# The expert loop's phase: the way down first, and the last block's hidden rows turned inside the way down before it

## The reference, cut to what matters

```python
x = x + concat(pool_mix(z), conv_mix(z)) @ w_out + b_out
h = rms_norm(x)
# the best of 4 expert groups, then the best 2 of its 8 experts; rows sorted into blocks of 128 per expert
yb = (silu(xblk @ w_eg[e]) * (xblk @ w_eu[e])) @ w_ed[e]      # per block: 128x1024 -> 512 -> 1024
y.at[buf_tok].add(yb * gate)
out = rms_norm(x + y)
```

## Time and profile before

| what | us |
|---|---|
| median of 3 runs | 1068.87 (1068.7 to 1072.86) |
| the profiled execution, its own time | 1070.19 |
| its span in the trace | 1068.4 |
| PE busy | 945.7 (89%) |
| DVE busy | 865.0 (81%) |
| ACT busy | 635.7 (59%) |
| POOL busy | 293.1 (27%) |

### The profile page before, as it was taken

How to read it: one execution, slowest core, us unless ns; L and a number is a source line. 1 busy time by engine, 2 the same in 40 slices (tenths; PEclk the granted TensorE clock), 3 DMA queues, 4 the chain that set the end, 5 groups by cost and what they waited for, 6 DMA issues and landing times.

```text
span 1068.4 us, 13431 instructions
## 1 busy us (share of the span) xinstructions
PE 945.7 (89%) x4446; PEld 774.7 (73%) x4446; DVE 865.0 (81%) x967; ACT 635.7 (59%) x623; POOL 293.1 (27%) x324
## 2 busy tenths in 40 slices
PE   4999999896898783969999999999999999999920
PEld 3888888574687563758888888888888888888720
DVE  6289998969756646889889898989898989898658
ACT  7244453563531103648787878787878787878515
POOL 2178688375153101002121212121212121212010
PEclk8999999897998875879999999999999999999965
DMA  8221111121351142579999999999999999999877
GB/s 265 82 61 40 40 40 45 37 104 45 133 217 60 69 153 90 214 262 368 379 377 390 389 391 383 402 384 384 384 392 372 384 384 374 380 385 384 296 248 273
DMA packets 67531, 268.63 MB, mean 251 GB/s; under 512 B 15359, under 2 KB 28159, under 8 KB 42921
## 3 DMA queue, kind: packets, MB, share of 16 engines
q1 hardware_dynamic: 57993, 250.36, 63.0%
q0 software_dynamic: 9504, 17.85, 4.4%
HBM read 254.09 MB, written 30.86 MB: 267 GB/s over the span
## 4 chain that ended last, share of the span: by engine, by line
PE 84%; DVE 6%; ACT 3%; DMA 3%; issue 3%; POOL 1%; SPq 0%; DVEq 0%; POOLq 0%; ACTq 0%
PE ps L1076 11%; PE ps L1074 11%; PE ps L1075 11%; PE ps L925 8%; PE ps L1088 6%; PE ps L1090 6%; PE ps L1089 6%; PE ps L801 5%; PE ps L802 5%; PE ps L803 5%; PE ps L1063 3%; PE ps L980 2%; PE ps L1095 1%; PE ps L839 1%; DMA arena<-hm_scratch,g_idx 1%
## 5 line engine op out<-in xcount | busy, mean ns | idle before, releaser
L726 ACT ACTIVATE big<-arena 128x2048 fp32r<-128x2048 f32 x192 | 362.5, 1913 | 70.4 <-PE ps L1090 38.6
L1525 DVE TENSOR_TENSOR low<-arena,big 128x2048 fp32r<-128x2048 f32 x126 | 285.2, 2285 | 39.8 <-ACT big L726 39.8
L1074 PE MATMUL ps<-big,ring 128*128 128x512 f32 x512 | 204.4, 399 | 2.4 <-DVE ring L1530 2.4
L1076 PE MATMUL ps<-big,ring 128*128 128x512 f32 x512 | 202.4, 395 | 0.0
L1525 DVE TENSOR_TENSOR big<-arena,big 128x2048 fp32r<-128x2048 f32 x66 | 151.0, 2289 | 16.5 <-ACT big L726 16.2
L1208 DVE SCALAR_TENSOR_TENSOR ps<-arena,cols,ps 128x512 f32<-128x512 f32 (+1 forms) x174 | 137.2, 788 | 6.0
L925 PE MATMUL ps<-big,ring 128*128 128x512 f32 (+1 forms) x432 | 113.4, 423 | 14.0 <-DVE ring L1274 7.1
L1074 PEld LDWEIGHTS ps<-big,ring 128*128 128x128 f32 x512 | 96.9, 189 | 22.1 <-DVE ring L1530 2.8
L925 PEld LDWEIGHTS ps<-big,ring 128*128 128x128 f32 (+1 forms) x432 | 84.6, 199 | 38.6 <-DVE ring L1274 7.5
L1076 PEld LDWEIGHTS ps<-big,ring 128*128 128x128 f32 x512 | 96.9, 189 | 21.2
L1088 PE MATMUL ps<-big,hT 128*128 128x512 f32 x256 | 103.0, 402 | 10.1 <-DVE hT L1540 10.1
(11 more groups left out here) (240 smaller groups left out, 1394.7 us busy)
## 6 DMA issues: line engine op xcount, KB each, us to landing
arena<-in_w_eg SPq DMA_DIRECT2D x64, 1024.0 KB, 7.5
arena<-in_w_eu SPq DMA_DIRECT2D x64, 1024.0 KB, 7.2
arena<-in_w_ed SPq DMA_DIRECT2D x64, 1024.0 KB, 7.6
arena<-in_x_prompt SPq DMA_DIRECT2D x16, 512.0 KB, 4.5
y_in<-y_scratch SPq DMA_DIRECT2D x16, 512.0 KB, 7.8
arena<-in_w_in SPq DMA_DIRECT2D x12, 512.0 KB, 3.6
arena<-in_w_out SPq DMA_DIRECT2D x8, 512.0 KB, 3.9
x_scratch<-arena SPq DMA_DIRECT2D x8, 512.0 KB, 2.6
```

The lines of the kernel that those rows point to most:

```text
L726: act.activation(we_h[n % RING], raw[n % RING], ACT.Copy).then_inc(high_done, 1)
L1074: pe.matmul(out, part_h[b][:, k, :], wh[:, q, :], start=(k == 0), stop=False)
L1076: ins = pe.matmul(out, part_l[b][:, k, :], wh[:, q, :], start=False, stop=(k == KD - 1))
L1525: dve.tensor_tensor(we_l[n % RING], raw[n % RING], we_h[n % RING].bitcast(F32), ALU.subtract).then_inc(low_done, 1)
```

## The change

PE's loop is rotated. A half round now begins with the way down of block p-1 and ends with up of block p+1; the way down of block 0, which stood ahead of the loop, is now the first thing in it, and that of the block before the last, which was the last thing in the loop, now follows it. Between its halves the last block's hidden rows are turned. Their copies go to a second buffer, `hT2`, in the region `hTr`, and ACT makes its copy before it copies the result of the block before. The ninth tile of x moves from `hTr` to the buffer of the gathered rows, `xe`, so its load waits for the last gather and its turning. The count `ye_done` gets one more at the start, on ACT ahead of its loop, and POOL and PE count one further. No arithmetic is added or removed, and the order of PE's work before the last turning is the same.

```diff
@@ -106,6 +106,9 @@
+        hT2_h = hTr[:, 0:FF].rearrange("p (k n) -> p k n", k=KF)
+        hT2_l = hTr[:, FF:2 * FF].rearrange("p (k n) -> p k n", k=KF)
@@ -162,7 +165,7 @@
         x_in = [raw[2 + t // 2][:, (t % 2) * D:(t % 2 + 1) * D] for t in range(NT - 1)] + [
-            place("x_last", AT_HTR, D)[:, :]]
+            xe]
@@ -484,7 +487,8 @@
                 if t == NT - 1:
-                    sp.wait_ge(ix_done, 2)
+                    sp.wait_ge(xe_tr, 2 * rest + 3)
+                    sp.wait_ge(gath, 32 * rest + 48)
                 elif t % 2 == 0:
                     sp.wait_ge(low_done, upto(rest, 2 + t // 2 - RING))
@@ -734,9 +738,9 @@
-            def hidden_high(blk):
+            def hidden_high(blk, to=hT_h):
                 act.wait_ge(h_tr, blk + 1)
-                act.activation(hT_h, h_ps, ACT.Copy).then_inc(h_high, 1)
+                act.activation(to, h_ps, ACT.Copy).then_inc(h_high, 1)
@@ -771,14 +775,17 @@
+            act.sem_inc(ye_done, 1)
             rest = pair_loop(act, body)
             ago = 2 * rest
             high(rest, 0)
             silu(ago + 1, upto(rest, 1 - RING))
             hidden_high(ago)
             high(rest, 1)
+            act.wait_ge(ix_done, 2)
+            hidden_high(ago + 1, hT2_h)
             result(ago, upto(rest, 5 - RING))
-            hidden_high(ago + 1)
             result(ago + 1, upto(rest, 1))
@@ -1076,7 +1083,7 @@
-            def expert_out(i, n, half):
+            def expert_out(i, n, half, hT_h=hT_h, hT_l=hT_l):
@@ -1115,13 +1122,15 @@
             slot_table("over", 0, 2 * NT)
-            pe.wait_ge(h_low, 1)
-            expert_out(-1, 10, 0)
-            expert_out(-1, 11, 1)
 
             def body(i, overflow):
                 for b in (0, 1):
                     at, prev = RING * b, 2 * i + b + 1
+                    pe.wait_ge(h_low, prev)
+                    pe.wait_ge(ye_done, prev)
+                    expert_out(i, at - 2, 0)
+                    expert_out(i, at - 1, 1)
                     pe.wait_ge(xe_low, prev + 2)
                     pe.wait_ge(silu_done, prev + 1)
                     expert_in(i, at, gate_ps)
@@ -1132,20 +1141,19 @@
                     turn_rows(prev + 2)
                     expert_in(i, at + 2, up_ps)
                     expert_in(i, at + 3, up_ps)
-                    pe.wait_ge(h_low, prev + 1)
-                    pe.wait_ge(ye_done, prev)
-                    expert_out(i, at + 4, 0)
-                    expert_out(i, at + 5, 1)
 
             rest = pair_loop(pe, body)
             prev = 2 * rest + 1
+            pe.wait_ge(h_low, prev)
+            pe.wait_ge(ye_done, prev)
+            expert_out(rest, -2, 0)
             pe.wait_ge(act_done, prev + 1)
-            pe.wait_ge(h_low, prev)
             turn_hidden(prev)
+            expert_out(rest, -1, 1)
             pe.wait_ge(h_low, prev + 1)
-            pe.wait_ge(ye_done, prev)
-            expert_out(rest, 0, 0)
-            expert_out(rest, 1, 1)
+            pe.wait_ge(ye_done, prev + 1)
+            expert_out(rest, 0, 0, hT2_h, hT2_l)
+            expert_out(rest, 1, 1, hT2_h, hT2_l)
@@ -1535,9 +1543,9 @@
-            def hidden_low(blk):
+            def hidden_low(blk, to=hT_l, high=hT_h):
                 dve.wait_ge(h_high, blk + 1)
-                dve.tensor_tensor(hT_l, h_ps, hT_h.bitcast(F32), ALU.subtract).then_inc(h_low, 1)
+                dve.tensor_tensor(to, h_ps, high.bitcast(F32), ALU.subtract).then_inc(h_low, 1)
@@ -1580,7 +1588,7 @@
-            hidden_low(ago + 1)
+            hidden_low(ago + 1, hT2_l, hT2_h)
@@ -1769,7 +1777,7 @@
             def store_rows(blk, copies):
-                pool.wait_ge(ye_done, blk + 1)
+                pool.wait_ge(ye_done, blk + 2)
```

## The result

The changed kernel takes 1078.0 us (median of 8 runs, 1075.57 to 1081.45) against 1070.65 for the kernel before (8 runs, 1067.41 to 1077.67). The ratio is 1.0065, with a 95% interval of 1.0042 to 1.0089: slower by 4.5 to 9.5 us. The prediction was 1069.8, in a range up to 1072.8, and wrong. As a change it was +0.9, and about +7.0 was measured.

The account below looks back on a forecast made before the run. PE bounds the loop; behind it the second row's first addition plus a fixed tail sets the time. Loop and entry 0, end +0.7, exit under load +0.2: together +0.9, put on the median 1068.87 as 1069.8, range 1066.9 to 1072.8.

Parts of the forecast that it names:

- The loop: PE's 15 rounds: nothing gets cheaper and the back edge costs nothing in its new place; 0, bounds 0 and 0.56 us per edge.
- rival B: Back edge bare in its new place, each round paying up to 0.56 us; 7.8 us more, 1077.6; chance 0.04.
- The loop's entry: Ahead of block 0's way down: entering the loop is covered by PE's wait for the hidden rows, 8.62 us before; 0.
- The exit under load: PE's loop exit, now among the loads of x: its code fetch or a shorter lead costs a little more; +0.2 us.
- The bound of 5.1: Upper bound for the exit's extra cost under load: what load does to a scatter, 8.3 - 3.2 = 5.1 us.
- Rival C: The fetch at PE's loop exit is slow: the exit's term grows by 2.5 to 5.1, 1072 to 1075; chance 0.10.
- The other theory for the exit: PE's lead over the array is shorter with 24 matmuls since the transposes instead of 48; can uncover some 2.5 us.
- The turning between the halves and the copies into `hT2`: Behind the exit: four transposes take 0.43 us; the copies, about 2.0, are ready while the second half runs.
- The wait for `ye_ps` in place of that for `hT`: Ahead of the last way down: PE waits for ACT's result copy; start 1016.74 against 1017.01, only 0.27 us gained.
- The clock of the last way down: Last way down at full clock, 5.73 us instead of 7.39, ending 1.93 earlier; other bound 0.27 earlier.
- The end: First row's loads start 0.99 us later, bound by bandwidth; second row's first addition 0.66 to 0.99 later, taken as +0.7.
- The two chains: Last scatter to second row's loads, and previous block's scatter to first row's nine additions; meet within 0.4 us at the end.

Follow-up runs that it names:

- e2: The changed kernel with SP's nine loads of x held until the first half of the way down of the block before the last is done; 1078.07 us, ratio 1.0068.
- e3: The kernel before with the nine loads of x held until the last block's gate is done, so under way at its exit; 1072.48 us, ratio 1.0015.
- e4: The changed kernel with PE's number of rounds read before its loop and PE's tail put right behind the loop; 1073.82 us, ratio 1.0019.
- e1: The kernel before with only the rotation: hidden rows turned behind both halves, hT and x's ninth tile unmoved; 1076.08 us, ratio 1.0049.
- e5: The kernel before with only PE's tail right behind its loop and the number of rounds read ahead of it; 1069.65 us, ratio 1.0007.
- e8: The changed kernel with PE's number of rounds read ahead of its loop, the far jump at the exit kept; one run, 1074.99 us.
- e6: The changed kernel with the near tail, SP holding the second row's loads until the first row's eighth load has landed; 1074.18 us, ratio 1.0042.

## Why the prediction was wrong

- The loop, 0: right. 500.00 of 500 us and 2350 matmuls again, and no bare back edge (rival B is out).
- The loop's entry, 0: right in kind. PE's wait there is 8.7 us, as the earlier trace rows.
- **The exit under load, +0.2: this is the step that failed.** It was sized near its lower end, "since two short packets are little beside 0.5 MB". It is +3.85 on the step (4.64 against the 0.79 that the sum already held), plus some 1.7 at the lower clock, which the sum didn't have at all behind this gap. e2 and e3 show that it is the load: 4.64 to 0.80 without the loads of x, 0.79 to 3.85 with them in the kernel before. The bound of 5.1, read off a scatter under load, held it. The argument against it looked at the size of the packets, while what counts is when one comes: it lasted 1.24 us instead of 0.96, but started 1.86 us behind the last matmul of the loop instead of 1.78 ahead. Rival C, at 0.10, was this case in kind; its 1072 to 1075 left out the clock and the slower loads.
- The other theory for the exit that I carried, that PE's lead over the array shrinks with 24 matmuls since the transposes, is out: e2's exit has the same 24 and a step of 0.80.
- The turning between the halves and the copies into `hT2`, covered: right. e4 shows them bare: the way down's halves and the transposes take what was worked out, and the copy of the result comes 6.5 us behind up, 0.4 later than before.
- The wait for `ye_ps` in place of that for `hT`: right, 1.77 from last to first matmul against the 1.67 worked out.
- The clock of the last way down: right. 19.07 to 24.91 is 5.84 with no matmul at the lower level. What I missed is that the clock would fall elsewhere.
- **The end, +0.66 to 0.99 for the loads: the second term that was too small.** I took the nine loads as bound by bandwidth and unmoved by what is issued behind them. They took 20.0 instead of 17.9, and the addition came 22.1 behind the first load instead of 19.7. e4, free of the exit, is 33.6 where this sum gives 31.6. The two chains were within 0.4 us of each other, as read; but the earlier trace rows name the DMA as what the addition waited for, so before it was the last scatter's chain that ended last. The load that I let land "in time" came 2.0 us behind the ninth in the changed kernel and in e4.

From up to the end the sum had 0.99 for the first load. With 3.85 + 1.66 + 2.39 more it is 8.9, and 8.9 was measured there in the profiled executions (4.5 to 9.5 by the ratio of all runs). The forecast's 0.9 was that 0.99, with 0.3 off for a load that lands in time and 0.2 on for the exit under load.

The Trainium skill's rule on taken branches to a page that isn't held ("Runtime: NRT & Kernel Launch", Instruction fetch mechanics) pointed the right way. This case adds the number: PE's step across the exit is 0.8 us when the DMA queues are idle, and 3.8 to 4.6 when they are full. In e1 the gap stood behind the first matmul of the new code, so here it was a page that came late and not the branch alone.

## What to carry to other kernels

Moving work across the end of a loop moves the loop's exit too. Look at what the DMA queues do at the new place: in this case the exit's code came through them, and a gap of half a microsecond behind an idle stretch can be four in a busy one, and bring the clock down as well. Putting the code that follows right behind the loop, and the rare part far away, takes the gap away in both places (e4, e5).

When two chains meet at the end, shortening one of them may buy nothing: here the last way down ended 2.4 us earlier in e4 and the kernel was no faster. Its scatter and the loads behind it then ran among the loads of the other chain. The second row's first load was issued 1.7 us earlier behind up than before, and landed 2.4 us later, 2.0 behind the ninth load of the first row.

## What the runs showed of the hardware that I had not expected

- PE's step across the same exit is 0.79 or 3.85 us (before, e3), 4.64 or 0.80 (after, e2), by nothing but when the loads of x are issued.
- Queue q8 moves no packet from 495 to 1005 us, while PE goes round its loop, in any of the kernels. Its next packet, of 16 KB, ends 1.5 to 1.6 us ahead of PE's first instruction behind the exit, whether it comes early (before, e2) or late (after, e3, e8); in e4, where PE doesn't stall, none stands between 1004 and 1014. So q8 carries PE's code.
- A load of 512 KB from the result scratch lands some 4.5 us behind its issue with nothing or little ahead of it (4.56 for the first and 4.46 for the second row's first in the kernel before), and 8.98 when it stands behind four others (after). The nine land after 18.0 us when the next nine are held back (e6), and after 19.4 when they are not (e4), in one trace each.
